# The HGRN layer of a two-block transformer as one row of 112 levels, prepared a unit ahead

## The reference, cut to what matters

```python
q, z_f, z_b, v, g = jnp.split(h @ w_in, 5, axis=-1)
q = silu(q)
logf = logaddexp(log(lb), log1p(-lb) + log_sigmoid(z2))   # for z_f and for z_b reversed in time
k2 = (1 - lb) * sigmoid(-z2)
# causal, per direction: o[t] = sum over s <= t of (q[t] * exp(B[t] - B[s]) * k[s]) . v[s],  B = cumsum(logf)
o = out[:, :, 0] + out[:, ::-1, 1]                        # both directions
o = o * rsqrt(mean(o * o) + EPS) * gn_g * silu(g)
return o @ w_out
```

## Time and profile before

| | |
|---|---|
| time of the profiled execution | 2410.43 us |
| its span in the trace | 2408.6 us |
| median of the three runs | 2412.55 us |
| TensorE busy | 2199.3 us (91%) |
| VectorE busy | 1476.7 us (61%) |
| ScalarE busy | 940.7 us (39%) |
| instructions | 26467 |

### The profile page before, as it was taken

The page is one execution under the profiler, slowest core; times in us unless marked ns, Lnnn a source line. Parts: engine busy times, 40 slices in busy tenths (PEclk is TensorE's granted clock), DMA queues, the critical chain, the costliest instruction groups (busy, mean ns, idle before and its releaser), DMA issues.

```text
span 2408.6 us, 26467 instructions
## 1 busy us (share of the span) xinstructions
PE 2199.3 (91%) x9974; PEld 1700.9 (71%) x9974; DVE 1476.7 (61%) x2690; ACT 940.7 (39%) x1720; POOL 13.0 (1%) x15
## 2 busy tenths in 40 slices
PE   4898998999899899889999998888888769999998
PEld 2665567776566776577888877777777657888886
DVE  6566665666255589866555554777777764433333
ACT  3334544344333343243223234555555533332331
POOL 1000000000000000000000000000000000000000
PEclk8998998999798799889999998999999879999998
DMA  7422212333222211034555541111111102323331
GB/s 294 157 105 70 69 66 62 128 131 110 69 71 94 99 62 53 18 131 140 184 194 181 183 157 44 44 44 44 45 44 44 44 3 68 106 96 96 97 96 53
DMA packets 65981, 228.73 MB, mean 95 GB/s; under 512 B 7104, under 2 KB 9280, under 8 KB 65728
## 3 DMA queue, kind: packets, MB, share of 16 engines
q1 hardware_dynamic: 65856, 227.05, 28.0%
HBM read 224.93 MB, written 2.10 MB: 94 GB/s over the span
## 4 chain that ended last, share of the span: by engine, by line
PE 66%; DVE 19%; ACT 7%; issue 4%; DMA 3%; SPq 0%; DVEq 0%; ACTq 0%
PE bank L377 17%; PE bank L379 17%; PE bank L378 17%; DVE arena L1556 5%; DMA w_raw<-weights_dram 3%; PE bank L1010 3%; PE bank L1033 2%; PE bank L679 2%; DVE arena L1786 2%; PE bank L1703 2%; DVE w_lo L315 1%; PE bank L1021 1%; DVE arena L1818 1%; DVE arena L1819 1%; ACT w_hi L306 1%
## 5 line engine op out<-in xcount | busy, mean ns | idle before, releaser
L377 PE MATMUL bank<-h_hi,w_hi 128*128 128x512 f32 (+1 forms) x1616 | 670.5, 415 | 60.6 <-DVE h_lo L646 20.4
L379 PE MATMUL bank<-h_hi,w_lo 128*128 128x512 f32 (+1 forms) x1616 | 643.5, 398 | 0.0
L378 PE MATMUL bank<-h_lo,w_hi 128*128 128x512 f32 (+1 forms) x1616 | 642.4, 398 | 0.0
L315 DVE TENSOR_TENSOR w_lo<-w_raw,w_hi 128x1024 fp32r<-128x1024 f32 (+3 forms) x290 | 333.1, 1148 | 203.0 <-ACT w_hi L306 202.7
L306 ACT ACTIVATE w_hi<-w_raw 128x1024 fp32r<-128x1024 f32 (+3 forms) x293 | 292.2, 998 | 416.7 <-DMA w_raw<-weights_dram 243.5
L377 PEld LDWEIGHTS bank<-h_hi,w_hi 128*128 128x128 f32 (+1 forms) x1616 | 311.1, 193 | 147.7 <-issue 72.8
L379 PEld LDWEIGHTS bank<-h_hi,w_lo 128*128 128x128 f32 (+1 forms) x1616 | 310.1, 192 | 69.6
L378 PEld LDWEIGHTS bank<-h_lo,w_hi 128*128 128x128 f32 (+1 forms) x1616 | 311.8, 193 | 63.6 <-issue 4.1
L377 PE MATMUL bank<-a_hi_t,w_hi 128*128 128x512 f32 x512 | 203.1, 397 | 1.5 <-DVE a_lo_t L1484 1.5
L378 PE MATMUL bank<-a_lo_t,w_hi 128*128 128x512 f32 x512 | 203.0, 396 | 0.0
L379 PE MATMUL bank<-a_hi_t,w_lo 128*128 128x512 f32 x512 | 202.9, 396 | 0.0
(11 more groups left out here) (238 smaller groups left out, 2525.8 us busy)
## 6 DMA issues: line engine op xcount, KB each, us to landing
w_raw<-weights_dram SPq DMA_DIRECT2D x261, 512.0 KB, 4.3
ada_raw<-ada_dram SPq DMA_DIRECT2D x128, 512.0 KB, 3.6
arena<-ada_dram SPq DMA_DIRECT2D x8, 1024.0 KB, 16.6
w_raw<-weights_dram SPq DMA_DIRECT2D x16, 256.0 KB, 2.6
xT<-x_dram SPq DMA_DIRECT2D x1, 2048.0 KB, 10.1
out_dram<-xT SPq DMA_DIRECT2D x8, 256.0 KB, 2.2
tables<-tables_dram SPq DMA_DIRECT2D x1, 1536.0 KB, 19.8
w_raw<-weights_dram SPq DMA_DIRECT2D x8, 144.0 KB, 3.5
```

Source lines behind the costliest of these rows:

```text
L315: eng.tensor_tensor(WL[:, slot, 0:w], RAW[:, raw, 0:w], WH[:, slot, 0:w].bitcast(F32), ALU.subtract).then_inc(lower_half(n)[0], 1)
L377: nc.tensor.matmul(o, WH[:, slot, cols], self.hi(k), start=(k == 0), stop=False)
L378: nc.tensor.matmul(o, WH[:, slot, cols], self.lo(k), start=False, stop=False)
L379: last = nc.tensor.matmul(o, WL[:, slot, cols], self.hi(k), start=False, stop=(k == self.K - 1))
```

## The change

The eight heads and two directions become 16 units `u` = 2 * head + d, and their levels one row of 112, with one continuous pair of buffers, one semaphore per kind of event and one `Slot` for each level. In each slot the engines also do a fixed share of everything else:

- **Preparation a unit ahead.** The scan, the decays, and the cross-chunk scores of unit u + 1 are done during unit u; its gates are made during unit u - 1 or u.
- **Gates by logarithm and exponential.** With G1 = exp(-z): log f = ln(1 + lb * G1) - ln(1 + G1), and k = exp(ln(1 - lb) - (z + ln(1 + G1))). Silu becomes z * exp(-ln(1 + exp(-z))). One table set that holds both functions is loaded once. Inputs are held above -43.5.
- **Evacuation.** VectorE instead of ScalarE takes the projected tiles out of PSUM, with the clamp in the same instruction. The order of the first two tiles of a head is exchanged.
- **One bank for both directions.** All products with the values of a head accumulate in bank 6 or 7 by turns, cross-chunk ones in slot 5, the others in slot 0 of the next unit. The copy and the addition of directions go away, and Square reads PSUM.
- **Query decays** are spread over ScalarE copies with a scale in place of five VectorE instructions.
- **Projection quarters** stand in the slots as 1, 2, 1, 2, 2, 1, 1, ten in each unit, in two banks.
- **Last head.** The normed outputs of heads 0 to 6 are split into halves in the slots of head 7, and the output projection of two tiles (`outer=2`) begins there chunk by chunk; the eighth chunk and the other six tiles follow the end.

```diff
+        class Hgrn:
...
+            def evac(self, h):
...
+                    if t == 3:
+                        nc.vector.tensor_copy(places[t], bk[:]).then_inc(free.sem, 1)
+                    else:
+                        nc.vector.tensor_scalar(places[t], bk[:], self.LOWEST, None, ALU.max).then_inc(free.sem, 1)
...
+            def gate_act(self, act, u):
...
+                nc.scalar.activation(self.G1, self.head(h)["B"][:, d, :], ACT.Exp, scale=-1.0).then_inc(self.gate_exp.sem, 1)
...
+                nc.scalar.activation(self.G2, self.G1, ACT.Ln, bias=ones[:, 0:1], scale=1.0).then_inc(self.gate_log.sem, 1)
...
+                nc.scalar.activation(self.G1, self.G1, ACT.Ln, bias=ones[:, 0:1], scale=GAIN[:, 32 + h:33 + h]).then_inc(self.gate_log.sem, 1)
...
+            def gate_dve(self, dve, u):
...
+                nc.vector.tensor_tensor(K, B, self.G2, ALU.add).then_inc(self.gate_mixed.sem, 1)
...
+                nc.vector.tensor_tensor(B, self.G1, self.G2, ALU.subtract).then_inc(self.gate_mixed.sem, 1)
...
+            def score_pe(self, pe, u, p):
+
+                e = 8 * u + p
+                if e >= 2:
+                    pe.wait_ge(self.picked.sem, self.picked.at(e - 1))
...
+                    pe.wait_ge(self.ready.sem, self.ready.at(g + 1))
...
+        class Slot(Stage):
+
+            PARTS = (1, 2, 1, 2, 2, 1, 1)
...
+            def pe(self, pe):
...
+                if l == 0:
+                    self.part(pe, 0)
+                    if u:
+                        H.pv_own(pe, u - 1)
+                    H.score_pe(pe, u, 0)
+                    H.score_pe(pe, u, 1)
+                elif l == 1:
+                    self.part(pe, 0)
+                    H.score_pe(pe, u, 2)
+                    if d == 0:
+                        H.tokens_pe(pe, h)
+                    self.part(pe, 1)
+                else:
+                    H.score_pe(pe, u, l + 1)
+                    for i in range(self.PARTS[l]):
+                        self.part(pe, i)
+                    if l == 2 and d == 0 and h:
+                        H.sum_pe(pe, h - 1)
+                    if l == 5:
+                        H.pv_cross(pe, u)
+                    if l == 6 and u < 15:
+                        H.cross_pe(pe, u + 1)
...
             def dve(self, dve):
...
+                H, u, l, woven = self.H, self.u, self.l, self.woven
+                h, d, g = u // 2, u % 2, len(LEVELS) * u + l
+                if g + 1 < 16 * len(LEVELS):
+                    H.sub(dve, g + 1)
+                H.mult(dve, g)
+                if l == 0:
+                    if u:
+                        H.pick(dve, u - 1, len(LEVELS))
+                    if u < 15:
+                        H.scan(dve, u + 1)
+                elif l == 1:
+                    H.pick(dve, u, 0)
+                if l:
+                    H.pick(dve, u, l)
+                if d == 0:
+                    if h and l == 1:
+                        H.projected[h].evacuate(dve, 4)
+                        H.projected[h].dve_part(dve, 4)
+                    if l == 2:
+                        H.key_decay(dve, u + 1)
+                        H.query_decay(dve, u + 1)
+                    if h and l == 3:
+                        H.scale_dve(dve, h - 1)
+                    if h and l == 5:
+                        H.gate_out(dve, h - 1)
+                    if woven and l == 4:
+                        woven.evacuate(dve, 0)
+                        woven.dve_part(dve, 0)
+                    if woven and l == 6:
+                        woven.evacuate(dve, 1)
+                        woven.dve_part(dve, 1)
+                        H.gate_dve(dve, u + 2)
+                else:
+                    if woven and l == 1:
+                        H.times_sigmoid(dve, h + 1, "q")
+                    if woven and l == 2:
+                        H.key_decay(dve, u + 1)
+                    if woven and l == 3:
+                        H.query_decay(dve, u + 1)
+                        woven.evacuate(dve, 2)
+                    if woven and l == 4:
+                        woven.dve_part(dve, 2)
+                    if woven and l == 5:
+                        woven.evacuate(dve, 3)
+                        H.gate_dve(dve, u + 2)
+                    if l == 6:
+                        if woven:
+                            woven.dve_part(dve, 3)
+                        H.times_sigmoid(dve, h, "g")
...
+        class HgrnOpening(Stage):
...
+                nc.scalar.preload_act_table_set("natural_log_exp_and_others")
+                H.gate_act(act, 0)
+                H.sigmoid_act(act, 0, "q", 0)
+                H.sigmoid_act(act, 0, "q", 1)
+                H.key_act(act, 0)
+                H.sigmoid_act(act, 0, "q", 2)
+                H.chunk_act(act, 0)
+                H.exp(act, 0)
+                H.gate_act(act, 1)
+                H.spread_act(act, 0)
+                H.key_act(act, 1)
```

More of the change, by code:

```diff
@@ L164, in weight_tiles @@
             for h in range(8):
-                out += [tile_of(hg, 1024 * part + 128 * h) for part in range(5)]
+                out += [tile_of(hg, 1024 * part + 128 * h) for part in (1, 0, 2, 3, 4)]
             out += [tile_of(I["hgrn_w_out_2"][0], 128 * j) for j in range(8)]
@@ L1590, in conv_layer @@
             return n2
[L1592 to L1598, removed]
-            def act(self, act):
[L1601 to L1615, removed]
-            def dve(self, dve):
[L1618 to L1628, removed]
@@ new lines, in build, with chunk, first_tiles @@
+        class Begun(Project):
+            def chunk(self, pe, k):
+                for t in range(self.outer):
+                    if k == 0:
+                        pe.wait_ge(*lower_half(self.n0 + t))
+                        free_bank(pe, self.before[t])
+                    if t == 0:
+                        pe.wait_ge(self.chunks[k].sem, self.chunks[k].at(1))
+                    last = self.matmuls(t, (k,))
+                    if k == self.K - 1:
+                        last.then_inc(tile_done, 1)
+            def first_tiles(self, pe):
+                self.chunk(pe, self.K - 1)
@@ new lines, in build, with __init__, act, dve @@
+        class HgrnOpening(Stage):
+            def __init__(self, H):
+                self.H = H
+            def act(self, act):
+                H = self.H
+                act.wait_ge(H.bounds.sem, H.bounds.at(2))
+                nc.scalar.preload_act_table_set("natural_log_exp_and_others")
[9 more added lines that the diff above has]
+                H.key_act(act, 1)
+            def dve(self, dve):
+                H = self.H
+                H.gate_dve(dve, 0)
+                H.scan(dve, 0)
+                H.sub(dve, 0)
+                H.times_sigmoid(dve, 0, "q")
+                H.query_decay(dve, 0)
+                H.key_decay(dve, 0)
+                H.gate_dve(dve, 1)
@@ L1638, in pe, with __init__ @@
+        class HgrnEnd(Stage):
+            def __init__(self, H):
+                self.H = H
             def pe(self, pe):
-                pe.wait_ge(self.squared.sem, self.squared.at(1))
-                nc.tensor.matmul(bank[4][:], ones, self.SQ, start=True, stop=True).then_inc(self.summed.sem, 1)
+                self.H.pv_own(pe, 15)
+                self.H.sum_pe(pe, 7)
             def act(self, act):
-                act.wait_ge(self.head.o_ready.sem, self.head.o_ready.at(1))
-                nc.scalar.activation(self.SQ, self.head.OS, ACT.Square).then_inc(self.squared.sem, 1)
@@ L1645, in act @@
[L1645 to L1654, removed]
@@ L1833, in lower_bounds @@
+                self.H.square_act(act, 7)
+                self.H.root_act(act, 7)
+                self.H.high_act(act, 7)
+            def dve(self, dve):
+                self.H.pick(dve, 15, len(LEVELS))
+                self.H.scale_dve(dve, 7)
+                self.H.gate_out(dve, 7)
+                self.H.low_dve(dve, 7)
+        bounds_ready = signal("lb_exp").take(2)
         def lower_bounds():
-            s1, s2 = signal("lb_steps"), signal("lb_exp").take(1)
-            s1 = s1.take(9)
+            s1 = signal("lb_steps").take(10)
+            s2 = bounds_ready
@@ L1900, in hgrn @@
[L1900 to L1905 removed]
+            pj = Project(5, C, P, HH, HL, [], None, evac_engine="dve", chunks=n1.split, outer=3)
@@ new lines, in hgrn @@
+            H = Hgrn(bounds_ready)
+            pj.evac, H.projected[0] = H.evac(0), pj
+            weave((n1, 0, 0.1, C + 1, 2 * C + 2), (pj, 2, 1), (HgrnOpening(H), 2.5, 1), (Do(pe=lambda pe: H.cross_pe(pe, 0)), 4.5, 1))
+            out, pr = {}, None
+            for h in range(8):
+                if h < 7:
+                    woven = Interleaved(5, C, P, HH, HL, [], H.evac(h + 1), evac_engine="dve", banks=(0, 1) if h % 2 else (1, 0))
+                    H.projected[h + 1] = woven
+                else:
+                    woven = None
```

(6 more changed lines are left out.)

519 lines of the change are left out of this document (315 added, 204 removed).

## The result

The changed kernel takes 2320.53 us (median of four runs, 2316.41 to 2323.34) against 2411.85 of the kernel before on the same chip: a ratio of 0.9612, 95% interval 0.9595 to 0.9628, or 91 us. The forecast was 2337 in 2312 to 2372. The profiled execution took 2317.73 us with a span of 2315.9, 92.7 less than before.

The account below looks back on a forecast made before the run. The prediction held that no engine alone but how the queues meet bounds the layer. 1491.6 + 7 x 53.0 + 41.3 + 9.4 + 36.8 = 1950.1 against 2026.03, 75.9 us less: 2337 us, range 2312 to 2372.

Parts of the forecast that it names:

- my own case: Whole kernel: heads of 53.0 us give 2337 us, within 2320 to 2353, at a 62% chance.
- The head: Each of seven HGRN heads was to take 53.0 us, bounds 50.3 and 58.6.
- the larger ones sum to 51.8: In a head's slots, the larger of TensorE's and VectorE's load in each slot, summed: 51.8 us.
- hand-offs: In each head, an allowance of 1.2 us added to the 51.8 of the slots.
- TensorE's sum of 50.3: TensorE's work in a head after the change, from distances of starts: quarters, scores, cross and value groups, transposes and sum.
- full look-ahead: Rival, 6%: heads take only 50.3 us and the opening ends at 1487, giving 2315 us.
- VectorE's work: VectorE's load in a head after the change: 47.0 us, or 45.7 with evacuations at the SBUF row.
- Opening: Start of the layer: cross scores at 1490 us, bounds 1487 and 1499, and first level score at 1491.6.
- Last head: Head without projection quarters, its slots' larger loads: 26.9 for unit 14 and 14.4 for unit 15, together 41.3 us.
- End: From the last product to the projection's first matmul 9.4 us, against 12.98 before; then 36.8 for the rest.
- The table loads: Rival, 7%: Ln and Exp keep reloading tables, 4 us a head on the path, head 57, time 2365.
- VectorE sets the row: Rival, 20%: VectorE's heavy slots and the stop behind the root add up; head 56.5 us, time 2361.

Follow-up runs that it names:

- run 7: Changed kernel with scan and chunk Exps of the next unit moved to slot 5, its decays and spread to slot 6: 2360.93 us, ratio 0.9785.
- run 4: Changed kernel without the load of the common Exp and Ln table set, so each change between them loads a table: 2365.68 us, ratio 0.9799.
- run 1: Changed kernel with VectorE, in slots 2 to 6, picking the level ahead's score before making its own level's difference and products: 2361.42 us, ratio 0.9783.
- run 6: Changed kernel with ScalarE, not VectorE, evacuating the projected tiles of heads 1 to 7, ahead of the high half and without clamp: 2326.11 us, ratio 0.9632.
- run 2: Changed kernel with an extra, unread VectorE difference in slots 2 and 4 of every unit: 2327.9 us, ratio 0.9644.
- run 3: Changed kernel with an extra, unread VectorE difference in every slot, 14 a head: 2370.46 us, ratio 0.9830.
- run 10: Changed kernel with three quarter tiles before the first cross scores, a third output tile's chunks behind the last value products, last cross-score products in slot 3: 2306.70 us.
- run 8: Changed kernel with three quarter tiles before the first cross scores and a third output tile's first seven chunks in the last unit's slots 2 to 6: 2311.92 us.
- run 12: Changed kernel with both late preparation (slots 5 and 6) and no common table set: 2410.96 us, ratio 0.9989.

## Why the forecast was right, and where it was off

- **Direction and mechanism** held: queues that stopped for each other, not an engine's load, bounded the layer; after the change TensorE sets the heads, and where the preparation comes late, a load stands in ScalarE's queue or the look-ahead is cut, the stops are back (runs 7, 4 and 1).
- **The size** was forecast too small. 2320.53 us is 16.5 under the 2337, at the very edge of the span 2320 to 2353 that I gave my own case, and 5.5 above the 2315 of a rival that I gave 6%.
- **The head** was the mis-sized term. The step "the larger ones sum to 51.8 ... I add 1.2 for hand-offs and take 53.0" failed: seven heads took 355.1 us, 50.7 each, where 7 x 53.0 is 371. That is 15.9 of the 16.8 us between 75.9 forecast and 92.7 seen. TensorE's sum of 50.3 was right. Half of the 2.4 is the slot-by-slot maximum, half the hand-offs. With the look-ahead whole the head lies below the sum of the maxima, 50.6 against 51.8, so heavy slots of VectorE were absorbed; with it cut the head is 54.7 (run 1). The loads of the single slots were not measured. I gave "full look-ahead" 6%; it is what the heads do. For the hand-offs 0.3 us is left, the head less TensorE's sum of 50.3.
- **VectorE's work**: 47.0 forecast by distances, 47.9 busy. The evacuation took 0.674 us, against the 0.682 of the row taken as nearest; the row on SBUF, 0.417, was the wrong end. The Trainium skill's rule that float32 from PSUM runs at the plain rate ("VectorE: DVE Perf Modes", "Why PSUM operands drop a tier") agrees. Its use against the change does not: in run 6 the head is 0.8 longer, though the times alone do not tell the two apart.
- **ScalarE**: 30.4 forecast, 31.7 measured, since the functions that read a bias or scale from a tile took 0.72 (one pointer) and 0.82 (two), not 0.62, and the small scaled copies 0.39, not 0.3. The Trainium skill ("ScalarE: Activation LUTs", "What ACT_TABLE_LOAD costs") gives about 93 ns for each pointer operand, which fits these rows.
- **Opening**: the cross scores start at 1487.85, 2.1 before the 1490 forecast (1.1 of it had come before the layer, at the 5701st matmul), and yet the first level score starts at 1493.11, not 1491.6. Between them the cross scores took 2.6 us, not 1.64, and a quarter tile another 2.7, which the forecast had put into the head. Both ran at a low clock: TensorE had waited 6.47 us ahead of them, and from 1484.0 to 1494.2 the granted clock was 0.51, which the forecast left out.
- **Last head**: 1.64 + 41.3 forecast from cross scores to last product, 42.8 seen. The second profile of the same kernel has 41.8, so the fit to 0.2 us is in part luck.
- **End**: 9.4 forecast, 10.3 seen. The group of cross-score products ahead of the last score, 1.2, was missing; the other terms came out 0.3 shorter. From there to the last residual 36.8 forecast, 36.25 seen.
- **The table loads**, a rival at 7%, did not stay, but as an experiment they cost 4.8 us a head from the second on, the forecast's figure plus 0.8, and 12.3 outside the seven heads, which the forecast had not priced. The 2.7 us that the Trainium skill gives for a switch ("ScalarE: Activation LUTs", "What ACT_TABLE_LOAD costs") would have made ScalarE the bound; run 4 shows 12 us of busy time more for ten loads, 1.2 each.
- **VectorE sets the row** (20%) did not happen, but runs 2 and 3 put it 1.3 to 1.6 us away.

## What to carry to other kernels

Where queues are in order, first sum each engine's distances of starts over a period. In this kernel, with every product made one event ahead, the largest of these sums (50.3) came within 1% of the period (50.6), and the sum of each step's maximum (51.8) was too high. What an engine has free in total does not price a stall: ten table loads on a ScalarE with 19 us to spare cost 4.8 us a head, because they stand ahead of an instruction that others wait for. When a chain of small steps ends a stage, fill it with work that nobody waits for, placed behind the last instruction that someone does wait for (run 10), not ahead of it (run 8). And two edits that together bring back the old time have not thereby explained it: compare where the time went, not only how much (run 12).

## What the runs showed of the hardware that was not expected

Products in plain float32 and in fp32r follow each other without a gap: TensorE's records cover 50.60 of 50.60 us with 308 matmuls, while 92 VectorE and 67 ScalarE instructions run beside them. As records overlap, the distances of starts say more: their forecast sum, 50.3, leaves 0.3 us a head at most for waits that were already met, by estimate. The start of the layer, before any changed instruction, differs by up to 11.4 us between profiles of kernels that are alike up to there; in the two profiles of before and after, the granted clock ahead of it differs in places (from 640 to 680 us 0.87 and 0.95, from 200 to 240 us 0.79 and 0.83). That the clock accounts for all of that difference was not shown.
